# The last stage of a decoder layer: six value chunks kept back, weights split by pairs, buffers moved

## The reference, cut to what matters

```python
def block(xb):                      # 128 tokens at a time
    ...                             # 8 heads x 16 experts chosen for each token: eidx, gw
    u = exp_u[eidx]
    v = exp_v[eidx]
    a = jax.nn.gelu(jnp.einsum('td,thkd->thk', xb, u).astype(jnp.float32))
    return jnp.einsum('thk,thkd->td', (gw * a).astype(dt), v)
...
h = _layernorm(DN_ALPHA * h + _peer(h, ...), ln3_g, ln3_b)
```

## Time and profile before

| | |
|---|---|
| median of 3 runs | 1788.76 us (1787.02 to 1788.97) |
| the profiled execution, its own time | 1783.71 us |
| its span from first to last instruction | 1782.0 us |
| mean granted TensorE clock | 0.995 |
| TensorE busy | 1743.2 us (98%) |
| VectorE busy | 1294.5 us (73%) |
| ScalarE busy | 653.0 us (37%) |
| GpSimd busy | 433.2 us (24%) |
| first product of the v stage | 1172.36 us |
| last product of the v stage | 1761.84 us |

### The profile page before, as it was taken

The page is one execution under the profiler, slowest core; times in us unless marked ns, Lnnn a source line. Parts: engine busy times, 40 slices in busy tenths (PEclk is TensorE's granted clock), DMA queues, the critical chain, the costliest instruction groups (busy, mean ns, idle before and its releaser), DMA issues.

```text
span 1782.0 us, 25428 instructions
## 1 busy us (share of the span) xinstructions
PE 1743.2 (98%) x10420; PEld 1517.4 (85%) x10420; DVE 1294.5 (73%) x1831; ACT 653.0 (37%) x1049; POOL 433.2 (24%) x294
## 2 busy tenths in 40 slices
PE   7999999999999999999999999999999999999996
PEld 6888888788788899999999999977777777777774
DVE  6544555558594299889544474479999899999997
ACT  5334545434543200222100011144454454554453
POOL 1000122100010002111121211124555455555440
PEclk9999999999999999999999999999999999999998
DMA  9654433656328487999999999999999999999994
GB/s 354 243 186 174 157 126 135 283 189 235 143 103 346 195 352 283 355 387 392 386 421 421 420 421 418 422 372 414 421 421 421 422 421 420 421 420 417 421 405 154
DMA packets 81859, 583.35 MB, mean 327 GB/s; under 512 B 9632, under 2 KB 9696, under 8 KB 11792
## 3 DMA queue, kind: packets, MB, share of 16 engines
q1 hardware_dynamic: 52848, 374.37, 52.7%
q0 software_dynamic: 28896, 207.36, 28.7%
HBM read 573.73 MB, written 7.34 MB: 326 GB/s over the span
## 4 chain that ended last, share of the span: by engine, by line
PE 90%; DMA 5%; DVE 3%; ACT 1%; issue 1%; SPq 0%; POOL 0%; DVEq 0%; ACTq 0%
PE bank L1021 25%; PE bank L718 11%; PE bank L735 10%; PE bank L1082 6%; PE bank L1079 6%; PE bank L1080 6%; PE bank L1071 6%; PE bank L1069 6%; PE bank L720 6%; DMA slots<-in_stream 3%; PE bank L1036 2%; PE bank L958 1%; DMA rows<-in_peer_v,eidx 1%; DMA act_raw<-in_xT 1%; PE bank L825 1%
## 5 line engine op out<-in xcount | busy, mean ns | idle before, releaser
L1021 PE MATMUL bank<-h2T,slots 128*128 128x144 f32 x3744 | 468.7, 286 | 2.8 <-DMA slots<-in_stream 2.7
L1021 PEld LDWEIGHTS bank<-h2T,slots 128*128 128x128 f32 x3744 | 462.1, 190 | 3.7 <-ACT ga L1368 3.5
L718 PE MATMUL bank<-act_split,ring_hi 128*128 128x512 f32 x896 | 320.4, 402 | 9.5 <-DVE ring_lo L1476 9.2
L1465 DVE TENSOR_TENSOR ring_lo<-ring_raw,ring_hi 128x2048 fp32r<-128x2048 f32 x90 | 205.9, 2290 | 135.4 <-ACT ring_hi L1138 135.1
L1836 DVE SCALAR_TENSOR_TENSOR rows<-rows,hrow 128x2048 f32<-128x2048 f32 x112 | 255.9, 2285 | 33.3 <-DMA hrow<-h_classes 15.1
L720 PE MATMUL bank<-act_split,ring_lo 128*128 128x256 f32 x896 | 251.5, 281 | 0.0
L689 POOL DMA_INDIRECT rows<-in_peer_v,eidx x64 | 189.5, 2960 | 168.2 <-DVE hrow L1842 144.1
L718 PEld LDWEIGHTS bank<-act_split,ring_hi 128*128 128x128 f32 x896 | 169.4, 189 | 51.1 <-DVE act_split L1476 9.5
L1138 ACT CAST ring_hi<-ring_raw 128x2048 fp32r<-128x2048 f32 x90 | 171.9, 1909 | 89.2 <-PE bank L735 72.1
L689 POOL DMA_INDIRECT rows<-in_peer_u,eidx x64 | 126.5, 1977 | 267.3 <-DVE rows L1836 266.7
L720 PEld LDWEIGHTS bank<-act_split,ring_lo 128*128 128x128 f32 x896 | 170.2, 190 | 0.1
(11 more groups left out here) (305 smaller groups left out, 2877.6 us busy)
## 6 DMA issues: line engine op xcount, KB each, us to landing
slots<-in_stream SPq DMA_DIRECT2D x213, 1024.0 KB, 11.7
ring_raw<-in_stream SPq DMA_DIRECT2D x91, 1024.0 KB, 4.9
grown<-in_stream SPq DMA_DIRECT2D x32, 1024.0 KB, 11.5
front_slots<-in_stream SPq DMA_DIRECT2D x7, 1024.0 KB, 12.6
w<-in_w SPq DMA_DIRECT2D x4, 1024.0 KB, 9.0
spill_slots<-in_stream SPq DMA_DIRECT2D x4, 1024.0 KB, 12.5
gb<-in_ln_g POOLq DMA_DIRECT2D x3, 1024.0 KB, 11.9
gb<-in_ln_b POOLq DMA_DIRECT2D x3, 1024.0 KB, 14.6
```

The lines of the kernel that those rows point to most:

```text
L718: pe.matmul(bank[n % 2][:, :], hi[:, k * P:(k + 1) * P], act_split[:, k].rearrange("p c t -> p (c t)"), start=(k == 0), stop=False, skip_g ...
L1021: last = pe.matmul(bank[(N_U + k) % 2][:, 0:NU], u_slot(k)[:, ko * P:(ko + 1) * P], h2T[:, ko, :], start=(ko == 0), stop=(ko == KO - 1))
L1465: dve.tensor_tensor(ring_lo[:, r, :], ring_raw[:, r, :], ring_hi[:, r, :].bitcast(F32), ALU.subtract).then_inc(lo_ready, 1)
```

## The change

- **Ending.** KEPT goes from 3 to 6, so chunks 122 to 127 are kept back. TensorE does the rest products of all six first, chunk by chunk, then whole column 0 for all six, then the four folds, then whole columns 1, 2 and 3.
- **Norms.** Tile 1 is summed, normed and stored first, between add_whole(0) and add_whole(2); tile 0's mean, squares and scaling come last. SyncE's stores and ScalarE's squares change their order with it.
- **Buffers for the ending.** Chunks 124, 125 and 126 are rounded into buffers of their own (late_first, late_more), and the weights of pair 62 (chunks 124, 125) go to w_late. These overlay weights already used, so they wait for w_ready to reach LATE_AFTER = 59. Pair 63 goes to w_split's first places and chunk 127 to high_b, both once chunk 121 has been used. gb3 moves to memory of used weights.
- **Weights by pairs.** w_high and w_low split the weights of two chunks at once, before the rounding of the even one; w_high(c) waits until chunk c - 3 has been used. w_ready counts pairs, and GROWS_AFTER with it.
- **Addresses.** high_b starts 64 bytes later, the two grown slots 256 bytes later, late_first and late_more 64 bytes past what lies below them. high_b now overlaps the first 64 bytes of the weights, so the rounding of chunk 1 waits for the first pair.
- **Gathers.** in_chunks spreads its 100 rows over ENDING - 2 = 120 chunks.

```diff
-GROWS_AFTER = (11, 22)
-KEPT = 3
+GROWS_AFTER = (6, 11)
+KEPT = 6
 ENDING = CHUNKS - KEPT
+LATE = (124, 125, 126)
+LATE_PAIR = 62
+LATE_AFTER = 59
...
-    done = in_units(CHUNKS - 1) + min(rest, rest * (m + 1) // (ENDING - 4))
+    done = in_units(CHUNKS - 1) + min(rest, rest * (m + 1) // (ENDING - 2))
...
             low_slots = sb("low_slots", [P, RAW, 2048], F32R, c0)
+            sb("below_high_b", [P, 16], c=c0)
             high_b = sb("high_b", [P, 2048], F32R, c0)
+            sb("below_grown", [P, 48], c=c0)
...
-            gb3 = sb("gb3", [P, 2, D], c=c0)
+            sb("below_late", [P, 16], c=c0)
+            late_first = sb("late_first", [P, 2048], F32R, c0)
+            w_late = sb("w_late", [P, 2, W_COLS], F32R, c0)
...
+            gb3 = sb("gb3", [P, 2, D], c=c2)
+            sb("below_more", [P, 16], c=c2)
+            late_more = sb("late_more", [P, 2, 2048], F32R, c2)
...
+        def split_pair(c):
+
+            if c // 2 == LATE_PAIR:
+                return w_late[:]
+            r = 0 if c // 2 > LATE_PAIR else c % RW // 2 * 2
+            return w_split[:, r:r + 2, :]
...
             last = CHUNKS - 1
-            for c in range(ENDING, last):
-                pe.wait_ge(w_ready, c + 1)
+            for c in range(ENDING, CHUNKS):
+                pe.wait_ge(w_ready, c // 2 + 1)
                 pe.wait_ge(split_lo, c + 1)
                 for j in range(NQ):
-                    rest_products(c, j, False, False)
...
+                    ins = rest_products(c, j, False, c == last)
+                    if c == last:
+                        ins.then_inc(rest_done, 1)
+
+            def whole_column(j):
+
                 for c in range(ENDING, CHUNKS):
                     ins = whole_products(c, j, False, c == last)
                 ins.then_inc(v_bank, 1)
+
+            whole_column(0)
             for j in range(NQ):
                 pe.wait_ge(c_out, j + 1)
                 pe.matmul(bank[C_BANK + j][0:NS, :], fold[:], accC[:, j * 512:(j + 1) * 512], start=True,
                           stop=True).then_inc(back_ready, 1)
+            for j in range(1, NQ):
+                whole_column(j)
...
+                if m == 1:
+                    act.wait_ge(w_ready, 1)
...
+                elif m in LATE:
+                    act.wait_ge(w_ready, LATE_AFTER)
+                elif m == CHUNKS - 1:
+                    act.wait_ge(split_used, ENDING)
...
-                if c >= RW:
-                    act.wait_ge(split_used, c - RW + 1)
-                act.copy(w_split[:, c % RW, W_TWICE:W_TWICE + NS], weights(c)[:, P:ND])
-                act.copy(w_split[:, c % RW, 0:ND], weights(c)).then_inc(w_hi, 1)
+                if c // 2 == LATE_PAIR:
+                    act.wait_ge(w_ready, LATE_AFTER)
+                elif c // 2 > LATE_PAIR:
+                    act.wait_ge(split_used, ENDING)
+                elif c >= RW:
+                    act.wait_ge(split_used, c - RW + 2)
+                w = split_pair(c)
+                act.copy(w[:, :, W_TWICE:W_TWICE + NS], weight_pair(c)[:, :, P:ND])
+                act.copy(w[:, :, 0:ND], weight_pair(c)).then_inc(w_hi, 1)
...
             add_gathered()
+            add_whole(0)
             for j in range(NQ):
+                add_rest(j)
+            mean(1)
...
+            variance(0, 1)
+            st.settle()
+            add_whole(1)
+            for j in range(NQ):
+                last_scaled(0, 1, j)
+            for j in range(2, NQ):
                 add_whole(j)
             mean(0)
```

More of the change, by code:

```diff
@@ L405, in split @@
             lo = low_slots[:, b, :] if b < RAW else low_grown[:, b - RAW, :]
-            return (high_a[:], high_b[:], high_c[:])[c % RH], lo
+            if c in LATE:
+                return (late_first[:], late_more[:, 0, :], late_more[:, 1, :])[LATE.index(c)], lo
+            return (high_b[:] if c == CHUNKS - 1 else (high_a[:], high_b[:], high_c[:])[c % RH]), lo
         cand = pq[:, 0:8, 0:CANDS].rearrange("p h (r c) -> p h r c", c=RUN)
@@ L578, in _ @@
                 sp.dma_start(tile, a["stream"][S_V0 + c]).then_inc(landing, 16)
-            for n, t in enumerate((0, 1)):
+            for n, t in enumerate((1, 0)):
                 for j in range(NQ):
@@ L1068, in rest_products @@
                 rest = bank[C_BANK + j]
-                pe.matmul(rest[:, :], w_split[:, c % RW, W_PAIR:W_PAIR + P], hi[:, cols], start=first, stop=False,
+                pe.matmul(rest[:, :], split_weights(c)[:, W_PAIR:W_PAIR + P], hi[:, cols], start=first, stop=False,
                           skip_group_check=True)
-                return pe.matmul(rest[0:NS, :], w_split[:, c % RW, P:ND], lo[:, cols], start=False, stop=final,
+                return pe.matmul(rest[0:NS, :], split_weights(c)[:, P:ND], lo[:, cols], start=False, stop=final,
                                  skip_group_check=True)
@@ L1097, in _ @@
             last = CHUNKS - 1
-            for c in range(ENDING, last):
-                pe.wait_ge(w_ready, c + 1)
+            for c in range(ENDING, CHUNKS):
+                pe.wait_ge(w_ready, c // 2 + 1)
                 pe.wait_ge(split_lo, c + 1)
                 for j in range(NQ):
-                    rest_products(c, j, False, False)
[L1103 to L1108, removed]
-                whole_products(last, j, False, True).then_inc(v_bank, 1)
-            for j in range(NQ):
-                rest_products(last, j, False, True).then_inc(rest_done, 1)
-            for j in range(2, NQ):
+                    ins = rest_products(c, j, False, c == last)
+                    if c == last:
+                        ins.then_inc(rest_done, 1)
+            def whole_column(j):
                 for c in range(ENDING, CHUNKS):
@@ L1430, in _ @@
                     act.wait_ge(quad_out, DENSE_Q)
-                    for c in range(RH):
+                    for c in range(0, RW, 2):
                         w_high(c)
@@ L1438, in _ @@
             for m in range(CHUNKS - RH):
-                w_high(m + RH)
+                if (m + RH) % 2 == 0 and m + RH >= RW:
+                    w_high(m + RH)
                 split_high(m + RH)
@@ L2023, in _ @@
             for m in range(CHUNKS - RH):
-                w_low(m + RH)
+                if (m + RH) % 2 == 0 and m + RH >= RW:
+                    w_low(m + RH)
                 split_low(m + RH)
```

40 lines of the change are left out of this document (19 added, 21 removed).

## The result

The changed kernel takes 1790.71 us (median of 20 runs, 1787.49 to 1797.27), the kernel before beside it 1786.81 (20 runs, 1782.82 to 1790.54): a ratio of 1.0024, interval 1.0016 to 1.0032. That is 3.9 us slower, where the prediction had 5.3 us faster, and it is above the predicted range. Not all of these 5.7 us belong to the change: the v stage begins at 1174.87 here and at 1172.36 before, and the code ahead of it is nearly the same.

The account below looks back on a forecast made before the run. TensorE was held to set the pace, with VectorE and the DMAs nearly full. Pitch -4.5, tail -8.5, folds +3.6, idle time +4.5, rounding and last high_b chunk -0.4 gave -5.3 us: 1783.5 us, range 1779.5 to 1789.5.

Parts of the forecast that it names:

- T0: Moment TensorE leaves chunk 121 and the ending begins; 1734.48 before, forecast 1730.0.
- g: Start of VectorE's last gathered row before the ending; forecast T0 - 3.15 = 1726.85, with chunk 127 startable 16.76 us later.
- After: 1734.48 - 4.5 = 1730.0: Forecast of T0: the time before less the 4.5 us expected from curing high_b's pitch in the loop.
- So nothing in the loop: Claim that weights by pairs cost the loop nothing, the 0.65 us later rounding being covered by 3.9 us of slack.
- part 2: Weights by pairs: 0.65 us on ScalarE and 0.47 on VectorE a pair; VectorE's row before the ending starts about 0.6 later.
- Rival 4: The last gathered row before the ending is late; no gain at g = 1732.1, at worst +6.7 us; chance 0.10.
- the idle time ahead of the rest products: TensorE's waits in the ending for VectorE's low halves, before rest products of chunks 126 and 127; some 4.5 us in all.
- part 1: high_b 64 bytes on: its 41 chunks in the loop take 4.56 us instead of 4.67, gaining 4.5 us.
- rival 2: The address shift does nothing and high_b chunks keep 4.67 us; -0.7 us, 1788.1; chance 0.25.
- VectorE's queue and the tail: Ending: serial VectorE work behind g sets TensorE's pace; from last column to end 11.3 us in place of 19.8.
- Can the DMAs follow?: Loop: six chunks and five gathered rows need 27.4 us at 421 GB/s, TensorE wants 27.36; loss under 2 us in all.
- rival 3: DMAs pace the loop: VectorE waits for rows, TensorE for low halves, losing 2 to 4 us; 1786.8; chance 0.13.

Follow-up runs that it names:

- the run with one row less due: Changed kernel with the other ending order, gathered rows between the turn and chunk 117 due one chunk later; 1780.98 us, ratio 0.9958 to the kernel before.
- part 1 alone: Kernel before with only high_b 64 bytes on, grown slots 256 bytes on and gb3 moved; 1786.96 us against 1787.26, ratio 0.9993.
- the best kernel: Changed kernel with row 115 due later after the turn and whole products of columns 0 and 1 behind each rest; 1779.24 us against 1786.38, ratio 0.9956.
- the run with both: Kernel before with high_b moved and rows after the turn due one chunk later; 1783.79 us against 1786.38, ratio 0.9983.
- the first smoothed kernel: Changed kernel with rows 114, 115, 116, 117 due at m = 46 to 49; 1789.67 us against 1787.26 for the kernel before.
- the filled kernel: Changed kernel with whole products of columns 0 and 1 behind each kept chunk's rest products; 1782.71 us against 1786.38 for the kernel before, ratio 0.9986.

## Why the prediction was wrong

The sum had the end at 1776.7 of span; it was at 1787.7. The 11.0 us between are: 2.5 of a later v stage (chance), 4.9 of the loop (562.57 against 557.64), 1.5 by which the last gathered row was later than T0 - 3.15, 0.1 up to TensorE's start on chunk 127 (1752.66 against g + 16.76 = 1752.54), and 1.9 from there on. The 1783.5 us of the forecast were counted from 1788.76, the median of three runs; from the 1786.81 of twenty they would be 1781.5.

- **Failed: "After: 1734.48 - 4.5 = 1730.0"**, the loop's sum, in which the gathers' new divisor has no term. The prediction took from it only that the last row is due one chunk earlier. It also moves rows at every other place where the division rounds differently, and one of these is the turn to the v rows, where no spare row is loaded: 5.0 us, all of the pitch's 4.5. The divisor alone shows it (+4.3 us), and with the due rows moved back the stop is gone. The trace of before had the sign of it, a wait of 2.41 us for a row at 1406.98, but the prediction read the waits for gathered rows in the last windows alone. ("So nothing in the loop", said of part 2, holds: pairs alone cost nothing.) Rival 4 had the right resource, a late row, at the wrong place.
- **Failed: the half clock.** The idle time ahead of the rest products was well sized (forecast 4.5; 4.8 named in the rows), but its price was taken to end with it. 1.7 us in the ending came on top, at a granted clock of 0.50, and 1.4 of the loop's 5.0 are the same thing. Moving the one addition removes both the stop and this.
- **Mis-sized: g.** The last row began at 1735.78 = T0 - 1.66, not T0 - 3.15. The row ahead of it had waited 1.59 us for its DMA.
- **Right: part 1, as a pitch.** 4.56 us a chunk for all three buffers; rival 2 fell, and putting high_b back brings 4.66 back. As a gain in time it is not shown: of 4.5 us, the three pairs of kernels that differ by this shift (and little else) show 1.3, 2 and 1.1 us in their ratios, none of them clear of the noise. The Trainium skill's rule in "SBUF — State Buffer", section "Who interferes with whom", that TensorE's ports wait for nobody, doesn't cover what an address does to a product's pitch; the trace disagrees with reading it that way.
- **Right: part 2.** The pair's place on VectorE is 1733.58 - 1733.11 = 0.47, ScalarE's two casts of a pair take 0.62 for 0.65 forecast, and pairs alone cost nothing.
- **Right: VectorE's queue and the tail.** From g to the start of chunk 127's low half 1750.23 - 1735.78 = 14.45 us, forecast 14.32. The tail is 11.0 against 11.3. Tile 1's norm fitted with 3.4 us to spare.
- **"Can the DMAs follow?" was right for the even rate, and rival 3 came true in part.** The window of the run with one row less due holds 500 us of products without a gap at 421 GB/s, so six chunks and five rows do come in the time TensorE needs for six. But that is level, with nothing to make up a delay. (Nor was 421 "flat" in the kernel before: its windows of 50 us from 1250 on show 418 to 421.) Where a row is due for each chunk (at the turn, and wherever rows catch up) VectorE waits for rows and TensorE for low halves, as rival 3 says: 3.6 us in part 1 alone, 3.2 in the best kernel. In that even window the 436 of the Trainium skill ("SBUF — State Buffer", section "The DMA setup-cost knee") was not needed; no run here reaches it over a long window.

**What stays open** is how much of the pitch's gain one gets. With high_b moved, some executions run in part at 4.64 us a chunk and some don't, and I can't say which will. The later due rows were never run on the kernel before with high_b in its place, so the 3 us of the run with both are not divided between the two; the kernel before loses only 0.8 us at the turn, which bounds what the rows could give there.

## What to carry to other kernels

When a due time is given by a division, list it for each step before and after, and look at the steps with no spare buffer, not at the last one alone. Where the DMAs are full on average, a faster inner loop is held up wherever more than the average is asked of them. A stall of the matmul engine has two prices, its length and the half clock that can follow it, so an ending fed chunk by chunk should keep work that is already loaded (here the whole products) between the pieces that wait. An engine's small serial operation belongs behind the one that another engine waits for.

## What the runs showed of the hardware

- **A buffer's address changes the pitch.** 64 bytes more make the products on high_b 389 ns in place of 395 to 397, 4.56 us in place of 4.67 for a chunk. No other shift was run, and why 64 bytes do it is open: products on ring_lo, on multiples of 8 KB too, take 389 ns.
- **Two pitches for the whole stream.** With high_b moved, TensorE works at 4.56 or at 4.64 us for every chunk (0.228 or 0.232 for a product), at full granted clock and busy for all of each window. The pace is constant between stops and changes, if it does, at one; in two kernels it is 4.64 from the stage's first chunks on. It changed from 4.56 to 4.64 at a distance of 0.36 us between two products (part 1 alone) and at the stops of the first smoothed kernel; from 4.64 to 4.56 at the long stop of the filled one (chunk 50, 8.15 us); through the stops of other kernels it stays or returns. The rate of the DMAs doesn't tell the two apart: windows of 50 us at 4.64 show 413 to 422 GB/s and those at 4.56 the same, and part 1 alone has 413 at both (its two windows above). With high_b unmoved every profile shows one pattern only (4.56, 4.56 to 4.58, 4.66 to 4.67), and its sum for three chunks, 13.8 us, lies between 13.68 and 13.92. What decides between the two is not settled.
- **Half clock after a stop isn't set by its length alone.** The granted clock fell to 0.50, 1.2 of 2.4 GHz, after 4.18 us (changed kernel), 0.8 us after the end of a stop of 4.41 us (divisor alone), and after 2.58 us in the ending, where TensorE had been stopping every 2 to 3 us since 1739. The stage's start shows it as well. TensorE waits for its first chunk in all 14 profiles. The clock fell behind waits of 2.25, 2.51, 2.74 and 3.21 us, and chunk 0 took 6.24 to 6.26 us; it stayed at 1.00 behind waits of 2.64, 2.72, 3.19 and 3.24, and chunk 0 took 4.85. No length of the wait separates the two, and 1.4 us hang on it. A window of the run with one row less due, whose wait was 2.25 us:

```profile
1180.00:1182.00 2.00, 2.00 (x6) 1.43 (x5) 2.00 (x4) 0.51 (x1) 1.05 (x1) 0.50 1.00 418
```

Nor did it fall after 3.35 us in the filled kernel:

```profile
1414.89 0.47 PE L1106 MATMUL bank<-high_a,w_split 128*128 128x512 f32 x1 [3.35 <-DVE low_slots L2022]
1415.20 0.40 PE L1107 MATMUL bank<-high_a,w_split 128*128 128x512 f32 x1
```
